# Loading one expert's weights ahead of the ring, into memory that the merged stage has left

## What is computed

```
N_EXPERTS, TOP_K, EXPERT_DIM = 64, 6, 256

def block_fn(tok, wt, e):                       # one block of tokens of expert e
    gu = x_pad[tok] @ w_gate_up[e]              # 1024 x 512 weights, 2 MB
    h = silu(gu[:, :EXPERT_DIM]) * gu[:, EXPERT_DIM:]
    return (h @ w_down[e]) * wt[:, None]        # 256 x 1024 weights, 1 MB

routed = segment_sum(y_rows, row_tok)
gus = xt @ ws_gate_up
shared = (silu(gus[:, :256]) * gus[:, 256:]) @ ws_down
x = layer_norm(ALPHA * x + routed + shared)
```

## Time and profile before

| | |
|---|---|
| median of 3 timed runs | 1451.17 us (1449.71 to 1451.38) |
| the profiled execution | 1447.05 us, span of its instructions 1445.4 us |
| TensorE busy | 1287.2 us of the span (89%), granted clock 0.949 |
| VectorE, ScalarE, GpSimd busy | 449.9, 309.8, 283.9 us |
| DMA | 294.12 MB, mean 203 GB/s |
| weights of the experts | 128 and 64 transfers of 1024 KB, median 21.2 and 23.4 us from issue to landing |
| merged stage, experts' stage | about 558 to 833 us, 834 to the end |

### The profile page before, as it was taken

The page is one execution under the profiler, slowest core; times in us unless marked ns, Lnnn a source line. Parts: engine busy times, 40 slices in busy tenths (PEclk is TensorE's granted clock), DMA queues, the critical chain, the costliest instruction groups (busy, mean ns, idle before and its releaser), DMA issues. The chain is left out here.

```text
span 1445.4 us, 23188 instructions
## 1 busy us (share of the span) xinstructions
PE 1287.2 (89%) x8205; PEld 753.1 (52%) x8206; DVE 449.9 (31%) x893; ACT 309.8 (21%) x825; POOL 283.9 (20%) x359
## 2 busy tenths in 40 slices
PE   6999999999999996999999879997888788988880
PEld 5455555556554444888746744554343445544440
DVE  1545544544431742333235611111111111111106
ACT  1223331333131343222223101111111101111110
POOL 2201101110110602000000122333224222332232
PEclk8999999999999898999999989999999889999895
DMA  4451111113100203333682169999999999999984
GB/s 120 121 151 51 44 51 51 51 44 100 67 1 13 56 20 82 100 86 90 237 331 88 60 222 322 389 380 390 399 403 397 397 399 409 381 377 400 402 282 180
DMA packets 134618, 294.12 MB, mean 203 GB/s; under 512 B 13008, under 2 KB 82768, under 8 KB 118048
## 3 DMA queue, kind: packets, MB, share of 16 engines
q1 hardware_dynamic: 117824, 265.72, 48.9%
q0 software_dynamic: 15632, 25.47, 7.4%
q10 hardware_dynamic: 1104, 2.16, 0.5%
HBM read 278.83 MB, written 27.04 MB: 212 GB/s over the span
## 5 line engine op out<-in xcount | busy, mean ns | idle before, releaser
L1769 PE MATMUL bank<-expert_gu,gathered_xT 128*64 128x256 f32 x2048 | 262.4, 414 | 63.4 <-DMA expert_gu<-in_expert_w_gate_up_dram 59.3
L427 PE MATMUL bank<-xT,w_head 128*128 128x512 f32 x480 | 241.0, 613 | 1.2 <-PEq L85 1.2
L1769 PEld LDWEIGHTS bank<-expert_gu,gathered_xT 128*64 128x64 f32 x2048 | 156.3, 149 | 152.7 <-issue 43.9
L1929 DVE SCALAR_TENSOR_TENSOR hidden<-gate,slot_w,bank 128x128 f32<-128x128 f32 x64 | 22.2, 347 | 447.2 <-ACT gate L1894 447.2
L1776 PE MATMUL bank<-expert_down,hiddenT 128*64 128x512 f32 x512 | 123.7, 603 | 1.5 <-DMA expert_down<-in_expert_w_down_dram 1.2
L1685 POOL DMA_INDIRECT sum_rows<-expert_y,row_col x64 | 101.4, 1584 | 49.0 <-POOL row_col L1680 48.1
L427 PEld LDWEIGHTS bank<-xT,w_head 128*128 128x128 f32 x480 | 78.8, 190 | 48.5 <-issue 42.4
L1894 ACT ACTIVATE gate<-bank 128x128 f32<-128x128 f32 x64 | 17.8, 279 | 321.9 <-PE bank L1769 321.9
L605 POOL TENSOR_TENSOR LO<-LT_diagonal,level_blocks 128x256 f32<-128x256 f32 x48 | 38.2, 830 | 233.2 <-DVE LT_corner L771 233.2
L1402 DVE TENSOR_TENSOR w_lo<-w_tile,w_hi 128x1024 fp32r<-128x1024 f32 (+1 forms) x32 | 35.1, 1098 | 116.5 <-ACT w_hi L1302 116.5
L1680 POOL COPY row_col<-row_idx 128x1 int32 (+1 forms) x64 | 12.8, 200 | 274.2 <-ACT expert_y L1901 191.1
(11 more groups left out here) (329 smaller groups left out, 1869.5 us busy)
## 6 DMA issues: line engine op xcount, KB each, us to landing
expert_gu<-in_expert_w_gate_up_dram SPq DMA_DIRECT2D x128, 1024.0 KB, 21.2
expert_down<-in_expert_w_down_dram SPq DMA_DIRECT2D x64, 1024.0 KB, 23.4
w_head<-in_w_in_dram SPq DMA_DIRECT2D x32, 512.0 KB, 3.7
w_tile<-in_w_in_dram SPq DMA_DIRECT2D x16, 512.0 KB, 3.9
sum_rows<-zero_rows SPq DMA_DIRECT2D x2, 2048.0 KB, 11.7
w_tile<-in_w_branch_a_dram SPq DMA_DIRECT2D x8, 512.0 KB, 5.1
w_pair<-in_w_in_dram SPq DMA_DIRECT2D x6, 512.0 KB, 3.7
x_rows<-in_x_dram SPq DMA_DIRECT2D x4, 512.0 KB, 6.6
```

Source lines behind the costliest of these rows:

```text
L427: mm = nc.tensor.matmul(bank[:, :], w_head[:, g, c, :], xT[:, c, :], start=(c == 0), stop=(c == KC - 1))
L1769: mm = nc.tensor.matmul(bank[parts[a], 0:2 * P], x[:, c, part], halves[:, a, :, :], start=(c == 0), stop=(c == KC - 1))
```

## The change

Expert 60 gets a fifth slot outside the ring: its gate/up weights go to the memory of `xT`, its down weights to the second half of `shared_gu`. SyncE loads them at the end of the merged stage, when all four `sg_psum` have been raised. The ring serves the other 63: its loop runs to i = 14, and the last refill is written out for three slots, with the experts 61, 62 and 63 in slots 0, 1 and 2. TensorE's last turn takes the weights by `weights_at`: step 4 (expert 60) from slot 4, the steps 5 to 7 from slots 0 to 2. The products, their order and all other buffers are the same. `odd_sums` moves to the memory of slot 3.

```diff
+AHEAD = NE - GROUP
             x1_rows_out(TT - 1)
+            for g in range(4):
+                sp.wait_ge(sg_psum[g], 1)
+            T["load_gu"](sp, GROUP, AHEAD)
+            T["load_down"](sp, GROUP, AHEAD)
...
-    odd_sums = T["xT"][:, :, :].rearrange("p (t a) n -> p t (a n)", t=TT)
+    odd_sums = at("odd_sums", [P, TT, D], "dnl")
...
+    def weights_at(i, s, last):
+        k, now = block_at(i, s)
+        if last and s == GROUP:
+            return GROUP, 1
+        return (k - 1, now) if last and s > GROUP else (k, now)
...
-            with sp.Fori(1, NE // GROUP) as i:
-
-                for s in range(GROUP + 1):
-                    if s < GROUP:
-                        T["load_gu"](sp, s, GROUP * i + s, lambda: sp.wait_ge(h_psum[s], i))
+            def refill(i, first, n):
+                for s in range(n + 1):
+                    if s < n:
+                        T["load_gu"](sp, s, first + s, lambda: sp.wait_ge(h_psum[s], i))
                     if s:
-                        T["load_down"](sp, s - 1, GROUP * i + (s - 1), lambda: sp.wait_ge(y_psum[s - 1], i))
+                        T["load_down"](sp, s - 1, first + (s - 1), lambda: sp.wait_ge(y_psum[s - 1], i))
+
+            with sp.Fori(1, NE // GROUP - 1) as i:
+                refill(i, GROUP * i, GROUP)
+            refill(NE // GROUP - 1, AHEAD + 1, GROUP - 1)
...
             def gate_up(i, s, first=False, last=False):
                 k, now = block_at(i, s)
-                pe.wait_ge(gu_in[k], GU_PARTS * 16 * now)
+                w, loads = weights_at(i, s, last)
+                pe.wait_ge(gu_in[w], GU_PARTS * 16 * loads)
...
-                gate_up_products(ps[k % 2], xgT[:, s // 2 % 2, :, :], k, parts[s % 2]).then_inc(gu_psum[k], 1)
+                gate_up_products(ps[k % 2], xgT[:, s // 2 % 2, :, :], w, parts[s % 2]).then_inc(gu_psum[k], 1)
...
-        T["wgu"] = [at(f"expert_gu{k}", [P, KC, 2 * ED], n) for k, n in enumerate(("xh", "xl", "dnh", "dnl"))]
+        T["wgu"] = [at(f"expert_gu{k}", [P, KC, 2 * ED], n) for k, n in enumerate(("xh", "xl", "dnh", "dnl", "xT"))]
+        T["wdn"].append(at("expert_down4", [P, ED // P, D], "w_t", 8192))
-        T["gu_in"], T["dn_in"] = mem.sems("gu_in", GROUP), mem.sems("dn_in", GROUP)
+        T["gu_in"], T["dn_in"] = mem.sems("gu_in", GROUP + 1), mem.sems("dn_in", GROUP + 1)
```

More of the change, by code:

```diff
@@ L1786, in later @@
             def later(i, s, last=False):
-                k, now = block_at(i, s)
+                k, now = weights_at(i, s, last)
                 a = (s + 1) % 2
@@ L1804, in later, with gate_up @@
                         pe.wait_ge(over_xt_ready, j + 2)
-            def gate_up(i, s, first=False):
+            def gate_up(i, s, first=False, last=False):
                 k, now = block_at(i, s)
-                pe.wait_ge(gu_in[k], GU_PARTS * 16 * now)
+                w, loads = weights_at(i, s, last)
+                pe.wait_ge(gu_in[w], GU_PARTS * 16 * loads)
                 if s % 2 == 0:
@@ L1820, in hidden, with down @@
                 nc.tensor.transpose(ps[4][:, k % 2 * P:k % 2 * P + P], h[:, k % 2, :], ident[:, :]).then_inc(h_psum[k], 1)
-            def down(i, s, first=False):
+            def down(i, s, first=False, last=False):
                 k, now = block_at(i, s)
-                pe.wait_ge(dn_in[k], 16 * now)
+                w, loads = weights_at(i, s, last)
+                pe.wait_ge(dn_in[w], 16 * loads)
                 pe.wait_ge(ht_ready[k], now)
@@ L1828, in down @@
                     pe.wait_ge(y_ready[before], then_)
-                down_products(ps[6 + k % 2], hT[:, k % 2, :], k).then_inc(y_psum[k], 1)
+                down_products(ps[6 + k % 2], hT[:, k % 2, :], w).then_inc(y_psum[k], 1)
             def shared_down(t):
@@ L1849, in turn @@
                         pe.wait_ge(sd_done, 2 * s)
-                    gate_up(i, s, first and s < 2)
+                    gate_up(i, s, first and s < 2, last)
                     if not (last and s >= STEPS - 2):
@@ L1858, in turn @@
                     if not (first and s == 0):
-                        down(i, s - 1, first and s < 3)
+                        down(i, s - 1, first and s < 3, last and s > 0)
                     hidden(i, s, first and s < 2)
@@ L1869, in _ @@
             turn(TURNS - 1, last=True)
-            down(TURNS - 1, STEPS - 1)
+            down(TURNS - 1, STEPS - 1, last=True)
         @block.scalar
@@ L2005, in program @@
         front_start = nc.sbuf_base
+        region_xT = front_start - 4 * KC * SEQ
         branches = ctx.enter_context(ExitStack())
@@ L2049, in program @@
         run_phase(nc, attention_phase, T, ps, w_in)
-        region = {"front": front_start, "dnT": region_dnT, "aoT": region_aoT, "av": region_av, "qkT": region_qkT,
+        region = {"front": front_start, "xT": region_xT, "dnT": region_dnT, "aoT": region_aoT, "av": region_av, "qkT": region_qkT,
                   "bias": region_bias, "w_t": after_splits}
```

## The result

The changed kernel takes 1457.16 us (median of 6 runs, 1456.31 to 1457.37). Beside it the kernel before takes 1450.44 us (6 runs, 1448.73 to 1451.38). The ratio is 1.0041, 95% interval 1.003 to 1.0052: slower by 6.7 us. The forecast was 1452.2, "same", in a range that ended at 1456.8. I had called anything within 2.9 us "same", so by my own bound this is slower, and the range missed by 0.4 us. What happened was the mechanism of rival 1, at its upper bound.

A forecast was written before the change was run, and what follows sets the result against it. The prediction took transfers to bound the middle of the experts' stage and TensorE's products its nearly tied end. Start +1.6 and end -0.6 gave +1.0 us on the median 1451.17: 1452.2, range 1447.5 to 1456.8.

The forecast's parts named there:

- rival 1: End of the merged stage: POOL's drain waits for the gathers, net +3.1 us, 1454.3 (1453.2 to 1456.8); chance 0.30.
- What bounds the kernel: Experts' stage: transfers bind the middle, 976 to 1366 us; from 1366.7 nearly tied, TensorE's products the longer.
- The load that goes from the ring: End of the experts' stage: last down weights land 7.9 us earlier, but the last product gains only 0.6 us.
- rival 2: End of the experts' stage is bound by transfers like the middle, a whole slot returns: about 1444.5 us; chance 0.12.
- The wait and the issues on SP: End of the merged stage: SyncE's wait and three issues, about 1.2 us, hide under POOL's drain and cost nothing.
- (a) Over_x: Start of the experts' stage: the overflow tokens' gather lands later beside the load, +1.6 us, upper bound 2.8.
- (b): End of the merged stage: POOL's drain may wait for the last gather's landing; treated as a rival, chance 0.30.
- By bytes it comes to the same: Last gather at the merged stage's end: 20 rows of 4 KB per engine, each behind 8 KB, also give +3.7 us.
- Does a late start last?: Experts' stage to 1366 us: a late TensorE makes refills and saturation late, and nothing absorbs the delay.
- The sum: Whole kernel: profiled 1447.05 + 1.6 (start) - 0.6 (end) = 1448.05 us, so +1.0, and 1452.2 on the median.

The follow-up runs named there:

- the best version: Against the kernel before: expert 52 outside the ring, its load behind the overflow transposes, two gathers moved to the experts' stage; 1440.76 us, ratio 0.9934.

## Why the prediction was wrong

**What bounds the kernel.** Right. The shares of the middle didn't move, and the place at the end lay in slack.

**The load that goes from the ring: -0.6.** Right: no wait for weights is left ahead of the last product, and rival 2 is out. The changed trace alone can't give the size, since the granted clock moved 1.6 us in it; at equal clock three kernels with the change are 0.4 to 0.8 us shorter there than three without. The timed runs with the load behind the overflow transposes (0.1 to 4 us faster) agree with that and with more.

**The wait and the issues on SP: 0.** Right: the added issues take 1.2 us, and SyncE is done at 832.6, 11.4 us before GpSimd's drain.

**(a) Over_x: +1.6.** Not paid in the changed kernel, as a consequence of the step that failed (b). I let the load meet the over_x gather, and in the changed kernel it never did: the stage that issues this gather began at 845.6, when the last of the load had just landed (845.5), and it took 6.19 us. With the load at the start of the experts' stage the price is real, 2.35 us where I had said 1.6, within the bound of 2.8.

**(b) POOL's drain, left to rival 1: the step that failed.** The forecast held the drain's end at 833.1 whatever the gathers did, priced their delay at the boundary at nothing and even used the drain as cover for SyncE. The drain waited for them: it ended 6.1 us later after the first gather (16.26 against 10.16), and so did the next stage's start. I gave this 0.30 because of one row, the drain at the kernel's end that lasts 6.4 us longer than any work or transfer. That row shows only that a drain may have a floor of its own. It says nothing on whether a drain also waits for landings. The two times that agreed within 0.2 us, 832.9 and 833.1, were the better evidence. Over all thirteen traces the drain ends 0.37 to 0.59 us after the last packet of GpSimd's queue.

**The size of rival 1: +3.7, measured +6.1.** The upper bound, 6.2, was right and the middle wasn't. I took the median of gathers in the saturated stage, 8.9 us; the last gather here took 11.3. "By bytes it comes to the same" doesn't hold. 20 packets of 8 KB on each of 16 engines are 2.62 MB, and with the gathers' own 1.28 MB they need 9.8 us at 400 GB/s, where the gathers alone had 5.1 (827.5 to 832.6): +4.7 and not +3.7. And the turns were mis-counted: the earlier trace rows show 424 packets for these 1.28 MB, 26.5 turns for each engine and not 20, for packets of under 512 bytes take turns as rows do. 26.5 packets of 8 KB on each engine would be 3.47 MB, more than the load has. So nearly all of it goes first: as an estimate, 1.28 + 3.15 MB at 400 GB/s are 11.1 us, +6.0, and the last packet of GpSimd's queue came 6.0 us later (15.67 against 9.66).

**Does a late start last?** Right: 2.35 us at the first expert are 2.3 us at the last product.

**The sum.** Start 6.1 and end -0.6 make +5.5, within the measured 4.3 to 7.5. What stands between the sum and 6.7 is open. One candidate is the part behind the last product, 43.5 us after and 41.3 before, in one trace each. The odd sums' memory is not its cause (41.6 us with this edit alone, 41.2 with expert 52 and 41.1 in the best version, which both have it); it is 42.4 to 43.3 us in six of the other kernels and follows nothing that I changed.

## What to carry to other kernels

Before you fill idle transfers, look at which small transfers are in flight there and who waits for them: here packets took turns, so the bulk load cost them a turn of its own packets' size for each of theirs, however small those were, and the end of the stage, which drains GpSimd's queue, waited for them. In this kernel an extra buffer outside the ring was worth the transfer of one slot only if its content was used while the consumer was still waiting for the ring, and was held over the stretches in which the transfers had time to spare: it gave 0 at expert 4, 4.6 us at 20, 7.0 at 52 and about 2 (0.1 to 4) at 60. Two times that agree in the trace (a landing and a drain's end) are a tie to be priced in full until a row excludes it; a row in which a drain takes longer for another reason doesn't.

## What the runs showed of the hardware

GpSimd's drain at the end of a stage ended 0.37 to 0.59 us after the last packet of the DMAs that GpSimd had issued, over drains of 5.1 to 11.7 us, and didn't wait for a load that SyncE had in flight. Four gathers of 128 rows, 442 packets of 4 KB and 134 of 4 bytes in both traces, landed in 4.5 to 5.2 us alone and took up to 11.3 us beside 3.15 MB of weights in 256 packets of 8 KB and 256 of 4 KB. A packet of 4 bytes took a turn between two of 8 KB as a whole row did. And the same sixteen products behind a wait took 3.65 us at a granted clock of 1.00 and 5.28 at 0.69.
